# An S5 layer on one core: all 32 stacks of powers times b-bar made by GpSimd in a row, kept in DRAM and brought back

## The chip, the core and the metric

The kernel runs on one core of a Trainium2 chip. Its engines are TensorE (PE in the rows), VectorE (DVE), ScalarE (ACT), GpSimd (POOL) and SyncE (SP), which here only issues transfers. Each engine runs its own list of instructions in order and meets the others through semaphores. The metric is the device time of one execution in microseconds.

## What is computed

The reference is a two-block network on 256 latent and 256 context tokens of width 1024. The first block has an attention layer and then an S5 layer (a diagonal complex state space model, run in both directions), the second has two hybrid layers. The change touches the S5 layer alone:

```
# first_block, layer 1 (kind 1)
h = x * (1 + scale) + shift
pz = h @ s5_w_in[0];  p, z = split(pz)
y, yc = s5_mixer(p, pc, lam_re, lam_im, log_step, b_re, b_im, c_re, c_im, d, glu_w, glu_b)
x = layer_norm(alpha * x + gate * ((y * silu(z)) @ w_out[1]))
```

The mixer has 128 groups of 16 channels and 64 complex states in each direction. It discretises the diagonal matrix (a-bar) and the input matrix (b-bar). The kernel takes eight time steps at once: what eight inputs add to the state is a matrix whose blocks are the powers 7, 6, ... 0 of a-bar times b-bar. One such matrix for four groups, real and imaginary part, is called a stack here: 128 partitions x 1024 numbers, 512 KB. There are 32 stacks.

## The kernel before, in words

The program is written as stages with a method for each engine. `flow` calls the stages in one order for all engines, so the order of calls is each engine's own order. `e.mark(name)` notes, for the engine whose list is being written, the last operation that it has done so far (`self.own`). `wait_mark(name)` waits for the noted operation of all four of PE, ACT, DVE and POOL:

```
def wait_mark(self, name):
    if self.e is not None:
        for other in ("pe", "act", "dve", "pool"):
            if self.marks["plan"][name, other] is not None:
                self._ge(*self.marks["plan"][name, other])
```

The part that matters runs so. Attention ends at the mark `at1`. Then comes the output projection `OUT1` (16 x 8 tiles of weights, split into a high and a low part: ACT makes the high part, DVE the low part, PE multiplies three times), the layer norm `LN1`, and four pieces of unrelated weight work from `backlog` in each of its two gaps. Then the mark `ln1`, `Mod2` (the layer's input H), and the S5 flow, `S5.flow`.

In `S5.flow` ACT and DVE begin with `wait_mark("ln1")`. Eight projections `p0` to `p7` (two tiles of 8 + 8 matmuls 128x512 each) and sixteen tiles of `z` follow. After the first two projections the stacks are woven in two by two, in `halves(u)`: PE turns (transposes) stacks u and u + 1, does one tile of a projection (or of z, for u from 24), and then multiplies both turned stacks with the inputs (`enter`, 32 matmuls 128x64). ACT copies the turned stacks out of PSUM. For u below 16 DVE copies the product into the state buffer S, above that ACT does. SP ships each projection through DRAM into the layout that `enter` wants (`ship_sp`).

A stack takes six TENSOR_TENSOR instructions 128x512 (`stack`, line 88 for the instruction itself). GpSimd makes it, except that DVE makes the odd ones below 16 (`owner`). It lies in one of three buffers BS until PE has turned it. GpSimd loads the b-bar of each stack, 64 KB, from DRAM (`load_bb`), two buffers BB. The powers P and the factors SA are loaded once, after the mark `at1`.

When stacks 0 to 15 have entered, DVE runs the recurrence of the first half of the groups (`recur_dve`, 248 TENSOR_TENSOR 128x128 in a dependent row), and after stack 31 that of the second. After the last z tile the outputs leave, in four parts q (`leave`), with panels of tables from DRAM (`panels_sp`), and the gated linear unit follows.

Of the kernel before, what the change touches and what calls it, by code (L numbers as in the profile page):

```python
# [11 lines left out]
MUL, ADD, SUB, MAX, MIN = ALU.mult, ALU.add, ALU.subtract, ALU.max, ALU.min  # L12
# [152 lines left out]
def step(gen, n=1):  # L165
    for _ in range(n):
        next(gen, None)
# [12 lines left out]
def build(nc, I, out):  # L180
    ctx = ExitStack()
    with ctx:
# [50 lines left out]
        A = sb("A", AN)  # L233
# [350 lines left out]
        class Ada:  # L584
# [52 lines left out]
            dve = pool = none  # L637
# [85 lines left out]
        class Attention:  # L723
# [105 lines left out]
            pool = sp = none  # L829
# [211 lines left out]
        SS = S5(nc, I, dict(locals()))  # L1041
# [106 lines left out]
        def flow(e, on):  # L1148

            on(Load())  # L1150
            on(TurnIn())
            ada0, setup = on(ADA[0]), on(SS.setup)
            step(setup)
            step(ada0, 3)
            step(setup)
            step(ada0, 2)
            step(setup)
            step(ada0, 3)
            e.mark("mod1")
            on(Mod1())  # L1160
            for v in VTM:
                on(v)
            proj, backlog, tables = on(PROJ1), chain(ada0, *[on(a) for a in ADA[1:]]), on(SS.tables)
            setup = on(SS.setup2)
            for i in range(24):
                step(proj)
                step(setup)
                if i in (14, 19, 21, 23):
                    step(tables)
            on(PowersStored())  # L1170
            at = 0
            for g in range(4):
                for i, _ in enumerate(on(AT1[g])):
                    if i < 16 and g < 3:
                        step(proj)
                    else:
                        step(backlog)
                    if at % 7 in (0, 2, 4, 5):
                        step(tables)
                    elif at % 8 == 3:  # L1180
                        step(backlog)
                    at += 1
                if g == 2:
                    rest(tables)
                    on(TablesDone(SS))
            e.mark("at1")
            outp = on(OUT1)
            on(HalvesOO())
            rest(outp)
            ln = on(LN1)  # L1190
            step(ln)
            step(backlog, 4)
            step(ln)
            step(backlog, 4)
            e.mark("ln1")
            on(Mod2())
            SS.flow(e, on, backlog)
            e.mark("s5")
            on(HalvesG())
            rest(on(GLU))  # L1200
            rest(on(OUT2))
            rest(on(LN2))
            e.mark("ctx2")
            on(Ctx2())
            for L in LAYERS:
                L.flow(e, on, backlog)
            e.mark("end")
            on(FIN)
            e.mark("last")
# [48 lines left out]
class S5:  # L1258
# [5 lines left out]
    def __init__(self, nc, I, L):  # L1264
# [8 lines left out]
        def dram(name, *shape):  # L1273
            return nc.dram_tensor(name, shape, F32, kind="Internal").ap()

        self.scr = [dram(f"scr{i}", 131072) for i in range(2)]
        self.ptab, self.ctab = dram("ptab", 128, 3072), dram("ctab", 128, 128, 256)
        self.btab = dram("btab", 128, 128, 32).rearrange("g p f -> p g f")
        self.kf, self.xs = dram("kf", 128, 16, 240), dram("xs", 128, 4096)


# [18 lines left out]
        self.TM = A[:, 2560:2816].rearrange("p (x r g) -> p x r g", x=2, r=2)  # L1300
        self.P = A[:, 2816:5120]
        self.BB = [A[:, 5120 + 128 * i:5248 + 128 * i].rearrange("p (g r n) -> p g r n", g=4, r=2) for i in range(2)]
        self.BS = [[A[:, 5376 + 1024 * i + 512 * r:5888 + 1024 * i + 512 * r].rearrange("p (g j n) -> p g j n", g=4, j=8)
                    for r in range(2)] for i in range(3)]
        self.U1 = A[:, 8448:8960].rearrange("p (g j n) -> p g j n", g=4, j=8)
        self.U1D = A[:, 26368:26880].rearrange("p (g j n) -> p g j n", g=4, j=8)
        self.BM = [A[:, 8960 + 1024 * i:9984 + 1024 * i].rearrange("p (r g q) -> p r g q", r=2, g=4) for i in range(3)]
        self.US = [A[:, a:a + 2048].rearrange("p (g c) -> p g c", g=32) for a in (0, 12032, 14080, 16128)]
        self.S = [A[:, a:a + 8192].rearrange("p (s r g) -> p s r g", s=64, r=2) for a in (18176, 26368)]
# [5 lines left out]
        self.ZS = [X[:, m, 0:256] if m < 8 else A[:, 2816 + 256 * (m - 8):3072 + 256 * (m - 8)] for m in range(16)]  # L1315
        self.l_pp, self.l_bb = sig("landed_powers"), [sig(f"landed_bbar{i}") for i in range(2)]
        self.l_p, self.l_u = [[sig(f"landed_s5_{x}{i}") for i in range(n)] for x, n in (("p", 2), ("u", 4))]
        W = I["s5_w_in"][0]
        self.proj = [Lin(f"p{b}", W, 8, 256 * b, 256, lambda k: self.H[:, k, :], 512,
                         lambda k: [(self.dve_step, ("h2", k))], self.act_evac, act=self.project_act(b)) for b in range(8)]  # L1320
# [39 lines left out]
            sp.dma(self.US[q][s * 16:s * 16 + 16, 16 * i:16 * i + 16, :], src[s]).then_inc(self.l_u[q], b)  # L1360


    def owner(self, u):
        return "dve" if u < 16 and u % 2 == 1 else "pool"

    def stacked(self, u):
        return (self.dve_step if self.owner(u) == "dve" else self.pool_step), ("st", u)

    def load_bb(self, pool, u):

        if u == 0:
            pool.wait_mark("at1")
            pool.wait_ge(self.l_pt, "p")
            pool.wait_ge(self.l_bt, 1)
            pool.dma(self.P, self.ptab[:, 0:2304]).then_inc(self.l_pp, "p")
            pool.dma(self.SA, self.ptab[:, 2560:3072].rearrange("p (x r g) -> p x r g", x=2, r=2)).then_inc(self.l_pp, "p")
        elif u > 1:
            pool.wait_ge(*self.stacked(u - 2))
        pool.dma(self.BB[u % 2].rearrange("p g r n -> p g (r n)"), self.btab[:, 4 * u:4 * u + 4, :]).then_inc(self.l_bb[u % 2], u)

    def stack(self, v, u):

        if v.name == "pool":
            if u == 0:
                self.load_bb(v, 0)
            if u < 31:
                self.load_bb(v, u + 1)
        if self.owner(u) != v.name:
            return
        BR, BI = self.BS[u % 3]  # L1390
        U1 = self.U1 if v.name == "pool" else self.U1D
        s = self.pool_step if v.name == "pool" else self.dve_step

        def pw(r):
            a = self.P[:, 1152 * r:1152 * r + 1152].rearrange("p (k g) -> p g k", k=9)[:, 4 * u:4 * u + 4, 7::-1]
            return a.unsqueeze(3).to_broadcast([128, 4, 8, 16])

        def bv(r):
            return self.BB[u % 2][:, :, r, :].unsqueeze(2).to_broadcast([128, 4, 8, 16])

        v.wait_ge(self.l_pp, "p")
        v.wait_ge(self.l_bb[u % 2], u)
        if u > 2:
            v.wait_ge(self.tr_done, ("bt", u - 3))
        v.wait_own()
        v.tt(BR, pw(0), bv(0), MUL).then_inc(s)
        v.tt(U1, pw(1), bv(1), MUL).then_inc(s)
        v.wait_own()
        v.tt(BR, BR, U1, SUB).then_inc(s)
        t = v.own  # L1410
        v.tt(BI, pw(0), bv(1), MUL).then_inc(s)
        v.wait_for(t)
        v.tt(U1, pw(1), bv(0), MUL).then_inc(s)
        v.wait_own()
        v.tt(BI, BI, U1, ADD).then_inc(s, ("st", u))

    def turn_pe(self, pe, u):
        pe.wait_ge(*self.stacked(u))
        for r in range(2):
            p = self.PS.take(pe, ("bt", u, r), (self.act_evac, ("bm", u, r)))  # L1420
            for g in range(4):
                x = pe.tr(p[:, g * 128:g * 128 + 128], flat(self.BS[u % 3][r][:, g]), self.ident)
        x.then_inc(self.tr_done, ("bt", u))

    def turn_act(self, act, u):
# [175 lines left out]
                    ACT.Gelu_apprx_tanh).then_inc(self.act_step, ("gelu", q, t4))  # L1601

    def flow(self, e, on, backlog):
        own = {("ship", "sp"): self.ship_sp, ("stack", "pool"): self.stack, ("stack", "dve"): self.stack,
               ("turn", "pe"): self.turn_pe, ("turn", "act"): self.turn_act, ("enter", "pe"): self.enter_pe,
               ("enter", "act"): self.enter_act, ("enter", "dve"): self.enter_dve, ("recur", "dve"): self.recur_dve,
               ("before", "act"): self.before_act, ("before", "dve"): self.before_dve, ("panels", "sp"): self.panels_sp,
# [2 lines left out]
        def part(name, *a):  # L1610
            if (name, e.name) in own:
                own[name, e.name](e, *a)

        def halves(u, between):

            part("turn", u)
            part("turn", u + 1)
            between()
            for i in (u, u + 1):
                if i + 3 < 32:  # L1620
                    part("stack", i + 3)
                part("enter", i)

        if e.name in ("act", "dve"):
            e.wait_mark("ln1")
        for u in range(3):
            part("stack", u)
        projs, z = [on(p) for p in self.proj], on(self.z)

        def ahead(b):  # L1630

            if e.name == "sp":
                if b < 8:
                    rest(projs[b])
                else:
                    step(z, 2)

        ahead(0)
        ahead(1)
        u = 0  # L1640
        for b in range(8):
            ahead(b + 2)
# [23 lines left out]
        part("before", 1)  # L1666
        part("leave", 2)
        part("leave", 3)


def flat(a):
    return a.rearrange("p j n -> p (j n)")


class Setup:
# [387 lines left out]
class Layer:  # L2063


    def __init__(self, nc, I, L, l):
# [11 lines left out]
        nc0 = 512 - c0  # L2078
        W = I["w_in_2"][l]
        o = [0]  # L2080
# [853 lines left out]
```

## Time and profile before

| | us |
|---|---|
| median of 3 runs | 2636.81 (2636.36 to 2639.2) |
| the profiled execution | 2635.93 |
| its span in the trace | 2634.1 |
| PE busy in the span | 2220.4 (84%) |
| DVE, ACT, POOL busy | 1362.2, 906.9, 501.3 |

The span is what the trace shows from first to last instruction. The profiled execution is 1.8 us longer than it, and lies 0.9 us under the median of the runs. Times below are from the start of the span. The output projection begins at 588, the S5 flow at about 722, its last z tile ends at 1010, and its outputs have left at about 1122.

### The profile page before, as it was taken

The page shows a single profiled execution, that of the slowest core. Times are in us where ns is not written, and L with a number is a line of the kernel's source. Part 1 is how long each engine was busy: PE and PEld are TensorE (multiplying, and loading weights), DVE is VectorE, ACT ScalarE, POOL GpSimd, SP SyncE. Part 2 cuts the span into 40 slices and gives each one's busy share as a digit, 9 for nine tenths or more (in the row PEclk, how much of TensorE's full clock was granted, in tenths as well). Part 3 has the DMA queues.
Part 4 walks back from the last instruction along what each step waited for, and adds up shares of the span by engine and source line. Part 5 has one row for each costly group of instructions (what it writes and reads, how often), then busy time and mean ns, then how long its engine had stood idle before and what let it go on. Part 6 is the DMA issues. An engine that isn't in the chain of part 4 may idle for free.

```text
span 2634.1 us, 33814 instructions
## 1 busy us (share of the span) xinstructions
PE 2220.4 (84%) x13593; PEld 1674.5 (64%) x13593; DVE 1362.2 (52%) x2527; ACT 906.9 (34%) x1779; POOL 501.3 (19%) x457
## 2 busy tenths in 40 slices
PE   6878888779899775489788987879999977976998
PEld 5756666558556575389553443668888745545998
DVE  4648677553446999165334355453333223455554
ACT  3335454551212432154212344232222222344443
POOL 0047787311058950000000010000000000000000
PEclk8989999999899987699889987989999978887999
DMA  8254454793344329975322211223323442102553
GB/s 277 92 166 134 133 168 132 231 294 111 128 108 107 84 67 192 235 197 165 110 78 64 80 65 49 64 64 96 96 84 91 146 142 64 65 1 86 178 176 106
DMA packets 423666, 324.38 MB, mean 123 GB/s; under 512 B 65086, under 2 KB 411470, under 8 KB 422358
## 3 DMA queue, kind: packets, MB, share of 16 engines
q1 hardware_dynamic: 386452, 295.70, 38.7%
q10 hardware_dynamic: 34242, 16.92, 2.2%
q0 software_dynamic: 2816, 9.60, 1.1%
q8 instruction: 108, 1.77, 0.3%
q14 instruction: 48, 0.39, 0.1%
HBM read 292.42 MB, written 29.75 MB: 122 GB/s over the span
## 4 chain that ended last, share of the span: by engine, by line
PE 60%; DVE 14%; POOL 10%; DMA 6%; ACT 5%; issue 4%; SPq 1%; ACTq 1%; DVEq 0%; POOLq 0%
PE ps L119 58%; POOL A L88 9%; DVE A L88 3%; ACT A L115 3%; DMA wbuf<-ctab 2%; DVE R L88 2%; DVE A L102 2%; PE ps L122 2%; DVE A L105 1%; DVE A L92 1%; SPq L125 1%; DVE A L93 1%; POOL A L125 1%; DVE A L96 1%; DMA wbuf<-in_ada_w 1%
## 5 line engine op out<-in xcount | busy, mean ns | idle before, releaser
L119 PE MATMUL ps<-R,R 128*128 128x256 f32 (+1 forms) x3968 | 843.8, 335 | 42.6 <-ACT R L115 32.5
L119 PEld LDWEIGHTS ps<-R,R 128*128 128x128 f32 x3968 | 631.9, 194 | 125.5 <-ACT R L115 26.5
L119 PE MATMUL ps<-HR,R 128*128 128x512 f32 (+1 forms) x1984 | 562.4, 368 | 44.4 <-DVE R L88 33.2
L88 DVE TENSOR_TENSOR R<-wbuf,R 128x1024 fp32r<-128x1024 f32 (+2 forms) x304 | 333.0, 1104 | 367.6 <-ACT R L115 367.5
L119 PEld LDWEIGHTS ps<-HR,R 128*128 128x128 f32 x1984 | 354.0, 191 | 110.6 <-issue 43.9
L115 ACT ACTIVATE A<-ps 128x512 f32<-128x512 f32 (+4 forms) x400 | 210.2, 555 | 598.2 <-PE ps L119 422.1
L88 POOL TENSOR_TENSOR A<-A 128x512 f32<-128x512 f32 (+3 forms) x258 | 293.5, 1152 | 568.2 <-DVE A L96 304.3
L88 DVE TENSOR_TENSOR A<-A 128x128 f32<-128x128 f32 (+4 forms) x796 | 361.9, 485 | 63.3 <-ACT A L115 26.7
L115 ACT ACTIVATE R<-wbuf 128x1024 fp32r<-128x1024 f32 (+2 forms) x304 | 270.1, 894 | 293.8 <-PE ps L119 265.7
L119 PE MATMUL ps<-H,wbuf 128*128 128x512 f32 (+2 forms) x928 | 344.1, 530 | 22.1 <-DVE H L93 22.1
L119 PE MATMUL ps<-A 128*128 128x64 f32 (+10 forms) x1736 | 295.7, 371 | 31.1 <-DMA wbuf<-ctab 10.6
L119 PEld LDWEIGHTS ps<-H,wbuf 128*128 128x128 f32 (+1 forms) x928 | 182.1, 199 | 170.0 <-issue 146.1
L119 PEld LDWEIGHTS ps<-A 128*128 128x128 f32 (+3 forms) x1736 | 187.3, 189 | 97.1 <-issue 67.5
L122 PE MATMUL ps<-C,A 128*128 128x128 f32 (+1 forms) x663 | 107.2, 303 | 108.9 <-DVE A L92 35.1
L88 POOL TENSOR_TENSOR A<-X 128x576 f32<-128x576 f32 x128 | 165.5, 1313 | 105.1 <-ACT X L115 83.9
L122 PEld LDWEIGHTS ps<-C,A 128*128 128x128 f32 (+1 forms) x663 | 83.0, 157 | 126.1 <-issue 52.3
L125 POOL DMA_DIRECT2D A<-in_rope x3 | 1.8, 609 | 819.0 <-PE ps L119 471.0
L119 PE MATMUL ps<-A,C 128*128 128x256 f32 (+5 forms) x296 | 106.4, 510 | 51.6 <-ACT A L115 50.6
L88 DVE TENSOR_TENSOR A<-ps,A 128x256 f32<-128x256 f32 (+1 forms) x100 | 53.6, 536 | 134.1 <-PE ps L119 132.1
L115 ACT ACTIVATE R<-A 128x256 fp32r<-128x256 f32 (+1 forms) x108 | 50.1, 502 | 177.0 <-DVE A L88 176.9
L102 DVE RECIPROCAL A<-A 128x1 f32<-128x1 f32 (+4 forms) x120 | 98.4, 820 | 20.8 <-ACT A L115 18.3
L119 PEld LDWEIGHTS ps<-A,C 128*128 128x128 f32 (+2 forms) x296 | 44.6, 187 | 100.9 <-ACT A L115 60.4
(102 smaller groups left out, 1628.2 us busy)
## 6 DMA issues: line engine op xcount, KB each, us to landing
wbuf<-in_w_ada SPq DMA_DIRECT2D x48, 1024.0 KB, 6.8
wbuf<-in_ada_w SPq DMA_DIRECT2D x24, 1024.0 KB, 8.9
wbuf<-in_w_out SPq DMA_DIRECT2D x24, 1024.0 KB, 5.6
wbuf<-in_w_ffn_gate SPq DMA_DIRECT2D x22, 1024.0 KB, 5.4
wbuf<-in_w_ffn_up SPq DMA_DIRECT2D x22, 1024.0 KB, 5.4
wbuf<-in_w_ffn_down SPq DMA_DIRECT2D x32, 704.0 KB, 4.6
wbuf<-in_attn_w_in SPq DMA_DIRECT2D x20, 1024.0 KB, 7.0
ctab<-A ACTq DMA_DIRECT2D x64, 256.0 KB, 3.0
```

What stands on the lines that cost most here:

```text
L88: return self.op(lambda e: e.tensor_tensor(out, a, b, op))
L92: return self.op(lambda e: e.tensor_scalar(out, a, s1, None, op0))
L93: return self.op(lambda e: e.tensor_scalar(out, a, s1, s2, op0, op1))
L96: return self.op(lambda e: e.scalar_tensor_tensor(out=out, in0=a, scalar=s, in1=b, op0=op0, op1=op1))
L102: return self.op(lambda e: e.reciprocal(out, a))
L105: return self.op(lambda e: e.reduce_max(out, a, AX_X))
L115: return self.op(lambda e: e.activation(out, a, func, bias=bias, scale=scale))
L119: return self.op(lambda e: e.matmul(out, lhsT, rhs, start=start, stop=stop, skip_group_check=True))
L122: return self.op(lambda e: e.transpose(out, a, ident))
L125: return self.op(lambda e: e.dma_start(dst, src, allow_slow_non_contiguous=slow), 16)
```

## The change

GpSimd makes all 32 stacks in one row, `stacks(e)`, called straight after the mark `at1`, that is ahead of `OUT1` and of the mark `ln1` in its list. DVE makes none. Each finished stack is written to a DRAM tensor `bstab` by GpSimd's own queue (`spill_stack`, 512 KB); three buffers BS take turns, and a buffer is used again when its write has landed. SP brings the stacks back (`back_sp`, 512 KB each) into 13 places BL: eight in a part of A that is free then, and from stack 16 on five that lie over BS and P. `back_sp(0)` waits for the mark `ln1`; `back_sp(16)` waits for the writes of stacks 29, 30 and 31. Four stacks are asked for ahead. PE turns a stack when it is back. The rest of the flow is as it was.

```diff
             e.mark("at1")
+            if e.name == "pool":
+                SS.stacks(e)
             outp = on(OUT1)
...
+    def spill_stack(self, pool, u):
+        pool.wait_ge(self.pool_step, ("st", u))
+        pool.dma(self.bstab[u], self.BS[u % 3]).then_inc(self.l_bs[u % 3], u)
+
+    def stacks(self, pool):
+
+        pool.wait_mark("at1")
...
+        for u in range(32):
...
+            if u < 31:
+                self.load_bb(pool, u + 1)
+            pool.wait_ge(self.l_pp, "p")
+            pool.wait_ge(self.l_bb[u % 2], u)
+            if u > 2:
+                pool.wait_ge(self.l_bs[u % 3], u - 3)
+            if u:
+                pool.wait_own()
+            pool.tt(BR, pw(0), bv(0), MUL).then_inc(s)
+            pool.tt(U1, pw(1), bv(1), MUL).then_inc(s)
+            t = pool.own
+            if u:
+                self.spill_stack(pool, u - 1)
+            pool.wait_for(t)
+            pool.tt(BR, BR, U1, SUB).then_inc(s)
...
+            pool.tt(BI, BI, U1, ADD).then_inc(s, ("st", u))
+        self.spill_stack(pool, 31)
+
+    def slot(self, u):
+        return u % 8 if u < 16 else 8 + (u - 16) % 5
+
+    def back_sp(self, sp, u):
+
         if u == 0:
...
+            sp.wait_mark("ln1")
+        if u == 16:
+            for v in (29, 30, 31):
+                sp.wait_ge(self.l_bs[v % 3], v)
+        elif u >= 8 and u < 16:
+            sp.wait_ge(self.tr_done, ("bt", u - 8))
+        elif u > 20:
+            sp.wait_ge(self.tr_done, ("bt", u - 5))
+        sp.wait_ge(self.l_bs[u % 3], u)
+        sp.dma(self.BL[self.slot(u)], self.bstab[u]).then_inc(self.l_bl[self.slot(u)], u)
 
     def turn_pe(self, pe, u):
-        pe.wait_ge(*self.stacked(u))
+        pe.wait_ge(self.l_bl[self.slot(u)], u)
...
-                if i + 3 < 32:
-                    part("stack", i + 3)
+                if i + 4 < 32:
+                    part("back", i + 4)
...
-        for u in range(3):
-            part("stack", u)
...
         ahead(0)
         ahead(1)
+        for u in range(4):
+            part("back", u)
```

Where this moves instructions, the order of the built programs shows it. Lines with - are of before, with + of after. In brackets are the semaphores that an instruction waits for: `pool_step` counts GpSimd's operations, `landed_stack0` to `2` the writes of the stacks.

On ScalarE, at the start of the S5 flow: the row ahead is `Mod2`, the changed row is the first copy of projection `p0` out of PSUM.

```order
 L115 ACTIVATE X<-X 128x256 [waits dve_step] x16
-L115 ACTIVATE X<-ps 128x2x256 [waits act_step,mm_done,act_evac]
+L115 ACTIVATE X<-ps 128x2x256 [waits mm_done,act_step,pool_step,act_evac]
 L115 ACTIVATE X<-ps 128x2x256 [waits mm_done] x3
 L115 ACTIVATE A<-ps 128x512 [waits tr_done]
```

The instructions are the same; this one now waits for `pool_step` too.

On SyncE, at the same place: `wbuf<-in_s_w_in` are weights of the projections, `scr` is the DRAM tensor through which they are shipped.

```order
-L125 DMA wbuf<-in_s_w_in 128x8x256 [waits mm_done] x3
-L125 DMA scr<-X 256x1x256 [waits act_evac] x2
-L125 DMA A<-scr 16x16x64 [waits dve_step,pool_step,mm_done,landed_s5_p0]
-L125 DMA A<-scr 16x16x64 x7
+L125 DMA wbuf<-in_s_w_in 128x8x256 [waits mm_done] x2
+L125 DMA A<-bstab 128x1024 [waits pool_step,dve_step,landed_stack0,act_evac,mm_done]
+L125 DMA A<-bstab 128x1024 [waits landed_stack1]
+L125 DMA A<-bstab 128x1024 [waits landed_stack2]
+L125 DMA A<-bstab 128x1024 [waits landed_stack0]
```

Four stacks are fetched between the second and the third panel of weights, and the first of these fetches has the wait for the mark, which the first shipped load had.

On GpSimd, inside the row of stacks: stack 1 and the start of stack 2.

```order
 L125 DMA A<-btab 128x4x32 [waits pool_step]
-L125 DMA A<-btab 128x4x32 [waits dve_step]
+L88 TENSOR_TENSOR A<-A 128x512 [waits landed_bbar1]
+L88 TENSOR_TENSOR A<-A 128x512
+L125 DMA bstab<-A 128x1024
+L88 TENSOR_TENSOR A<-A 128x512 [waits pool_step]
+L88 TENSOR_TENSOR A<-A 128x512
+L88 TENSOR_TENSOR A<-A 128x512 [waits pool_step] x2
+L125 DMA A<-btab 128x4x32 [waits pool_step]
```

The wait for DVE's stack is gone, and a 512 KB write stands between the second and the third operation of each stack.

## Rows read from the trace of the kernel before

**Rows 1.** The page: the span, and the chain that ended last, by engine.

```profile
span 2634.1 us, 33814 instructions
...
PE 60%; DVE 14%; POOL 10%; DMA 6%; ACT 5%; issue 4%; SPq 1%; ACTq 1%; DVEq 0%; POOLq 0%
```

**Rows 2.** Stretches: engine busy us and counts, granted TensorE clock, DMA share.

```profile
core 0: us, PE busy (x) PEld busy (x) DVE busy (x) ACT busy (x) POOL busy (x), PEclk, DMA share, GB/s
588.40:722.00 133.60, 123.21 (x588) 89.47 (x588) 51.22 (x77) 33.28 (x66) 10.95 (x7) 0.93 0.38 119
...
746.00:843.00 97.00, 97.00 (x514) 66.39 (x513) 58.43 (x87) 21.86 (x41) 66.34 (x63) 1.00 0.40 100
843.00:958.70 115.70, 85.88 (x457) 64.56 (x455) 113.71 (x116) 50.43 (x80) 108.08 (x96) 0.88 0.29 76
1010.00:1060.00 50.00, 22.75 (x412) 18.83 (x416) 46.73 (x191) 14.65 (x15) 0.00 (x0) 0.66 0.99 216
```

**Rows 3.** Timeline of PE: start us, us, instruction, count, idle before and releaser.

```profile
716.82 29.11 PE L119 MATMUL ps<-H,wbuf 128*128 128x512 f32 x64 [8.44 <-DVE H L93]
745.76 1.91 PE L122 MATMUL ps<-C,A 128*128 128x128 f32 x16
747.51 7.03 PE L119 MATMUL ps<-H,wbuf 128*128 128x512 f32 x16
...
842.87 1.92 PE L122 MATMUL ps<-C,A 128*128 128x128 f32 x16
...
859.44 8.73 PE L119 MATMUL ps<-H,wbuf 128*128 128x512 f32 x16
...
909.31 3.62 PE L119 MATMUL ps<-H,wbuf 128*128 128x256 f32 x16
...
968.21 41.66 PE L119 MATMUL ps<-H,wbuf 128*128 128x256 f32 x192
...
1074.42 2.79 PE L119 MATMUL ps<-A 128*32 128x128 f32 x48 [7.47 <-DMA A<-ctab]
```

**Rows 4.** Waits of PE from 720 to 970: total us, times, longest.

```profile
PE ps L122 <- POOL A L88: 29.9, 8, 7.3
```

**Rows 5.** Timeline of GpSimd: stack 0, a b-bar load, stacks 17 and 18.

```profile
588.39 10.32 POOL L88 TENSOR_TENSOR A<-A 128x512 f32<-128x512 f32 x6 [7.22 <-DMA A<-btab]
599.01 0.79 POOL L125 DMA_DIRECT2D A<-btab  x1 [0.29 <-POOL A L88]
...
834.93 6.99 POOL L88 TENSOR_TENSOR A<-A 128x512 f32<-128x512 f32 x6
...
843.01 7.10 POOL L88 TENSOR_TENSOR A<-A 128x512 f32<-128x512 f32 x6
```

**Rows 6.** VectorE beside stack 0 (timeline), and its low parts from 600 to 700 (group).

```profile
588.32 3.50 DVE L88 TENSOR_TENSOR R<-wbuf,R 128x1024 fp32r<-128x1024 f32 x3
597.74 2.05 DVE L88 TENSOR_TENSOR R<-wbuf,R 128x1024 fp32r<-128x1024 f32 x1 [5.93 <-ACT R L115]
...
L88 DVE TENSOR_TENSOR R<-wbuf,R 128x1024 fp32r<-128x1024 f32 x12 | 14.7, 1226 | 26.6 <-ACT R L115 26.6
```

**Rows 7.** VectorE in two stretches of the recurrences: us, busy us, count.

```profile
846.00:958.00 112.00, 110.10 (x112) 0.88 0.28 75
995.00:1060.00 65.00, 60.77 (x248) 0.74 0.93 205
```

**Rows 8.** GpSimd's loads of powers, 560 to 960: count, busy us, mean ns.

```profile
L125 POOL DMA_DIRECT2D A<-ptab x2 | 1.1, 572 | 88.6 <-DVE A L88 88.6
```

**Rows 9.** DMA issues, 578 to 700, then 720 to 960: KB each, us to landing.

```profile
A<-btab POOLq DMA_DIRECT2D x3, 64.0 KB, 8.0
...
wbuf<-in_s_w_in SPq DMA_DIRECT2D x10, 1024.0 KB, 6.2
scr<-X SPq DMA_DIRECT2D x16, 256.0 KB, 2.5
A<-scr SPq DMA_DIRECT2D x64, 64.0 KB, 3.0
```

More of the change, by code:

```diff
@@ L1278, in __init__ @@
         self.btab = dram("btab", 128, 128, 32).rearrange("g p f -> p g f")
+        self.bstab = dram("bstab", 32, 128, 1024)
         self.kf, self.xs = dram("kf", 128, 16, 240), dram("xs", 128, 4096)
@@ L1302, in __init__ @@
         self.BB = [A[:, 5120 + 128 * i:5248 + 128 * i].rearrange("p (g r n) -> p g r n", g=4, r=2) for i in range(2)]
-        self.BS = [[A[:, 5376 + 1024 * i + 512 * r:5888 + 1024 * i + 512 * r].rearrange("p (g j n) -> p g j n", g=4, j=8)
-                    for r in range(2)] for i in range(3)]
+        self.BS = [A[:, 5376 + 1024 * i:6400 + 1024 * i] for i in range(3)]
+        self.BL = [A[:, a:a + 1024] for a in [26368 + 1024 * i for i in range(8)] + [5376, 6400, 7424, 2816, 3840]]
         self.U1 = A[:, 8448:8960].rearrange("p (g j n) -> p g j n", g=4, j=8)
-        self.U1D = A[:, 26368:26880].rearrange("p (g j n) -> p g j n", g=4, j=8)
         self.BM = [A[:, 8960 + 1024 * i:9984 + 1024 * i].rearrange("p (r g q) -> p r g q", r=2, g=4) for i in range(3)]
@@ L1317, in __init__ @@
         self.l_p, self.l_u = [[sig(f"landed_s5_{x}{i}") for i in range(n)] for x, n in (("p", 2), ("u", 4))]
+        self.l_bs = [sig(f"landed_stack{i}") for i in range(3)]
+        self.l_bl = [sig(f"landed_stack_back{i}") for i in range(13)]
         W = I["s5_w_in"][0]
@@ L1360, in ship_sp @@
             sp.dma(self.US[q][s * 16:s * 16 + 16, 16 * i:16 * i + 16, :], src[s]).then_inc(self.l_u[q], b)
[L1363 to L1367, printed above, removed]
     def load_bb(self, pool, u):
-        if u == 0:
[L1372 to L1415, printed above, removed]
@@ new lines, in load_bb, with pw, bv @@
+        if u > 1:
+            pool.wait_ge(self.pool_step, ("st", u - 2))
+        pool.dma(self.BB[u % 2].rearrange("p g r n -> p g (r n)"), self.btab[:, 4 * u:4 * u + 4, :]).then_inc(self.l_bb[u % 2], u)
+    def spill_stack(self, pool, u):
[3 more added lines that the diff above has]
+        pool.wait_mark("at1")
+        pool.wait_ge(self.l_pt, "p")
+        pool.wait_ge(self.l_bt, 1)
+        pool.dma(self.P, self.ptab[:, 0:2304]).then_inc(self.l_pp, "p")
+        pool.dma(self.SA, self.ptab[:, 2560:3072].rearrange("p (x r g) -> p x r g", x=2, r=2)).then_inc(self.l_pp, "p")
+        self.load_bb(pool, 0)
+        for u in range(32):
+            BR, BI = [self.BS[u % 3][:, 512 * r:512 * r + 512].rearrange("p (g j n) -> p g j n", g=4, j=8) for r in range(2)]
+            U1, s = self.U1, self.pool_step
+            def pw(r):
+                a = self.P[:, 1152 * r:1152 * r + 1152].rearrange("p (k g) -> p g k", k=9)[:, 4 * u:4 * u + 4, 7::-1]
+                return a.unsqueeze(3).to_broadcast([128, 4, 8, 16])
+            def bv(r):
+                return self.BB[u % 2][:, :, r, :].unsqueeze(2).to_broadcast([128, 4, 8, 16])
+            if u < 31:
[13 more added lines that the diff above has]
+            pool.tt(BR, BR, U1, SUB).then_inc(s)
+            t = pool.own
+            pool.tt(BI, pw(0), bv(1), MUL).then_inc(s)
+            pool.wait_for(t)
+            pool.tt(U1, pw(1), bv(0), MUL).then_inc(s)
+            pool.wait_own()
+            pool.tt(BI, BI, U1, ADD).then_inc(s, ("st", u))
+        self.spill_stack(pool, 31)
@@ L1421, in turn_pe @@
             for g in range(4):
-                x = pe.tr(p[:, g * 128:g * 128 + 128], flat(self.BS[u % 3][r][:, g]), self.ident)
+                a = 512 * r + 128 * g
+                x = pe.tr(p[:, g * 128:g * 128 + 128], self.BL[self.slot(u)][:, a:a + 128], self.ident)
         x.then_inc(self.tr_done, ("bt", u))
@@ L1603, in flow @@
     def flow(self, e, on, backlog):
-        own = {("ship", "sp"): self.ship_sp, ("stack", "pool"): self.stack, ("stack", "dve"): self.stack,
+        own = {("ship", "sp"): self.ship_sp, ("back", "sp"): self.back_sp,
                ("turn", "pe"): self.turn_pe, ("turn", "act"): self.turn_act, ("enter", "pe"): self.enter_pe,
@@ L1668, in flow @@
         part("leave", 3)
-def flat(a):
-    return a.rearrange("p j n -> p (j n)")
 class Setup:
```

## The prediction

> **What bounds the kernel now.** I read the page first: PE is on the chain that ended last for 60% of the span and GpSimd for 10% [rows 1]. 10% is some 260 us, as long as the S5 flow, so the flow was to be read by stretches and then engine by engine.
>
> The reader should see two regimes. From 746 to 843 PE is busy for all of 97.0 us [rows 2]: although the chain names GpSimd, PE has no idle time there. Turns of stacks 0 and 1 begin at 745.76 and those of 16 and 17 at 842.87 [rows 3], eight pairs in 97.1 us, 12.14 us a pair. Stacks made faster give nothing there. From 843 to 958.7 PE is busy for only 85.9 of 115.7 us [rows 2], and its waits for GpSimd sum to 29.9 us in 8 waits [rows 4]; the rest of what is lost is a lower clock after such waits (granted 0.88; a projection tile of 8.73 us where it takes 7.03) [rows 2, 3]. After that the last twelve z tiles end at 968.21 + 41.66 = 1009.9 [rows 3].
>
> The undisturbed length of the flow, from the first turn to the last z tile, is then 12 pairs with a projection tile at 12.14 (145.7), 4 pairs with a z tile at 12.14 - 7.03 + 3.62 = 8.73 (34.9) and 41.7 for the rest [rows 3]: 222.3 us. Before it took 1009.9 - 745.8 = 264.1. So **41.8 us** is all that stacks on time can give, if everything else stays. What follows (the outputs, paced by DMA: DMA share 0.99 from 1010 to 1060 [rows 2]) is chained behind the last z tile and moves with it.
>
> **What the change does to the order: the term that decides.** GpSimd's row of stacks stands in its list before the mark `ln1`. The mark notes each engine's last operation so far. Before, GpSimd's was the last operation of the tables: 2 memsets and 32 x 6 operations, count 194. Now it is the last operation of stack 31, count 194 + 192 = 386. Everyone who waits for `ln1` now waits for **all 32 stacks**: ACT ahead of its first copy out of PSUM in the flow, DVE ahead of its first copy, SP ahead of the first stack brought back, as the changed rows of ACT and SP in the section on the change show. Behind ACT's wait are queued all copies of projections and turned stacks; behind SP's the third panel and all shipping; PE waits for stack 0 to be back. PE can do the first four projection tiles (29.1 us from 716.8 [rows 3]) and then stands. Let G be the time when stack 31 is finished. Nothing in the flow goes on before G.
>
> **G, step by step.** Stack 0 starts at 588.39 as before and takes 10.32 us; the next b-bar load is issued from 599.01 for 0.79 us [rows 5], so stack 1 starts at 599.8. In an unbroken row the start-to-start time is 843.01 - 834.93 = 8.08 us (six operations 6.99, the rest one b-bar load with its gap) [rows 5]. Each further stack also issues a write. A load of 9 KB a partition took 0.57 us of GpSimd's issue [rows 8], a b-bar load with many small pieces 0.79 with 0.29 of gap [rows 5]. The write has one piece a partition, so I take 0.57 and a gap of 0.2: 0.78. Its lower end is 0 (hidden in the wait between operations 2 and 3), its upper 1.08. A stack is then 8.86 us (8.08 to 9.16). Stack 31 starts 30 x 8.86 = 265.8 later, at 865.6, and ends 6.99 + 0.78 later: 873.4 (849 to 883).
>
> To this comes VectorE's share of the memory. Stack 0 took 10.32 where another takes 6.99: 3.3 us more, beside 3.50 us of VectorE's low parts; at 597.74 it is VectorE that takes 2.05 for 1.23 [rows 5, 6]. So one waits for the other. Twelve more low parts of 1.23 us, 14.7 together [rows 6], now meet GpSimd, and in LN1 some dozens of short operations, which I put at the same again (an estimate: DVE's 51.2 busy us of 588 to 722 [rows 2] less the low parts and what reads PSUM). In the other direction stands 846 to 958, where VectorE did 112 operations in 112 us and GpSimd's stacks took 7.10, hardly more than 6.99 [rows 5, 7]: there VectorE paid. I take 14 us, half of the 29, with the ends 0 and 29. **G = 887** (849 to 912).
>
> The Trainium skill, page "SBUF — State Buffer", section "SBUF: two separate sides", says that VectorE operations with two SBUF inputs and GpSimd operations share one port pair, and that whichever starts first gets it for the whole instruction while the other fully blocks. This speaks against moving the stacks beside the low parts. By it GpSimd could lose the full 29 us and the time would be some 15 us above my forecast; the trace agrees in kind at stack 0 (3.3 us lost beside 3.50) but not in amount at the recurrences.
>
> **From G to the end.** The first stack comes back 512 KB later: 256 KB land in 2.5 us and 1 MB in 6.2 [rows 9], so about 3.7, after an issue of about half a us: turn 0 at G + 4. The first `enter` also needs the projections shipped, which used to run under the other projections: ACT's two copies and four issues of stacks ahead (G + 2), two writes that land behind 2 MB of stacks (to about G + 9), eight loads issued over 3.8 us and landed 3.0 later [rows 9]: G + 15.8, where PE would be ready at 4 + 1.9 + 7.0 = 13 (15 on the low clock). Call it 8 us from G to the point that answers to 745.8, with ends 4 and 14. Then 222.3 us: the last z tile ends at G + 230.3 = **1117**, against 1009.9: **+107.4 us**.
>
> What hides the rest. LN1's operations on VectorE get slower beside GpSimd by up to some 15 us, and PE's four projection tiles start so much later: covered, since PE has 887 - 746 = 141 us to spare. The low parts in `OUT1` are made while PE still multiplies earlier groups (three buffers); a wait for GpSimd of some 0.8 us each (2.05 for 1.23 [rows 6]) should be hidden, and if it were not, 12 x 0.8 = 10 us still lie within the 141. The recurrences: with GpSimd quiet, 248 operations take 65 us, where beside GpSimd 112 took 112 us [rows 7]. The first starts at G + 8 + 100 and ends at G + 173, the second starts after stack 31 has entered (about G + 190) and ends at G + 255; the outputs that need it start 64.5 us after the last z tile before (1074.42 - 1009.9 [rows 3]), here at G + 295. So it has 40 us of slack and gives nothing. DVE's eight stacks left out lie beside PE-bound work: nothing. The added transfers: 16 MB of writes at 0.5 MB in 8.9 us, and 16 MB back at 1 MB per pair of 12.1 us, some 85 GB/s on top of 100, below the 216 GB/s that were reached [rows 2]: nothing. `back_sp(16)`, which waits for stacks 29 to 31, finds them done.
>
> Sum: 2635.9 (the profiled execution) + 107.4 = **2743 us**, 4% above the median of 2636.8, which lies 0.9 us above that execution.
>
> **Rivals.**
> 1. The hold at `ln1` does not bite and the flow starts at 746 as before. For it speaks only that the text of the flow itself is unchanged; against it that the first rows of ACT, DVE and SP now wait for `pool_step`. Then `back_sp(16)` is the gate: stack 16 is back at G + 5 = 892 instead of turned at 843, then 222.3 - 97.1 = 125.2 us remain: 1017, +7 us, **2643**. With the lowest G of 849 it is 979, -31 us, 2605: this is the way to **faster**, and it gives faster if G is below about 875. The same holds if G itself were below 780 (then G + 230 < 1010), but that wants 5.8 us a stack, under the 6.99 of its operations alone.
> 2. GpSimd is throttled by its transfers. b-bar loads landed in 8.0 us while the large weight loads ran [rows 9]; a stack gives them 8.9. If the writes on the same queue push them to 11, some 12 to 14 stacks take 3 us more: +40, **2783**. A write itself has two stacks' time, 15 us.
> 3. GpSimd's writes cost nothing and VectorE always gives way: G = 849, **2706**.
>
> **How the numbers follow.** Forecast 2743: chance 0.80 with its own spread. Rival 1: 0.04, split between no change, faster and slower. Rival 2: 0.09. Rival 3, exactly at its end: 0.07. The ends are -24 to +9 for the writes (31 x the ends of 8.08 and 9.16 against 8.86), -14 to +15 for the port, -4 to +6 for the restart; taken together without adding all of one sign: 2715 to 2775. A difference of 0.2% (5 us) is about what a measurement of this kernel can tell from no change. Faster by more than that 0.02, within it 0.01, slower 0.97.
>
> **What would show it.** Right: GpSimd works without a gap from 588 to about 887; ACT has one idle time of over 140 us ended by GpSimd, PE one of about 130 ended by the stack brought back; after it the flow takes about 225 us with PE hardly waiting, pairs 12.1 us apart; the recurrences take 65 us each. Wrong: if ACT copies the first projection tile at 725 as before, the reading of the mark is wrong. If stacks are 8.1 or 9.5 us apart instead of 8.9, the size is off by 31 times the difference. If PE waits inside the flow for stacks brought back, the restart or the transfers were underrated.

## The result and the profile after

The changed kernel takes 2732.79 us (median of 4 runs, 2730.11 to 2736.5) against 2636.59 before: ratio 1.0367, 95% interval 1.0347 to 1.0388. It is 96 us slower. 2743 was forecast, with 2715 to 2775 as the range. The profiled execution took 2730.11, its span is 2728.3, 94.2 us longer than that of before [rows 1].

The page, the span and the chain that ended last by engine and by line:

```profile
span 2728.3 us, 33885 instructions
...
PE 61%; DVE 13%; POOL 12%; DMA 6%; ACT 4%; issue 2%; SPq 1%; ACTq 0%; DVEq 0%; POOLq 0%
```

ScalarE around the mark `ln1` (timeline: start, us, instruction, count, idle before and its releaser):

```profile
775.56 0.42 ACT L115 ACTIVATE X<-X 128x256 f32<-128x256 f32 x1 [2.56 <-DVE H L93]
874.52 2.06 ACT L115 ACTIVATE X<-ps 128x512 f32<-128x512 f32 x4 [98.55 <-POOL A L88]
```

This is the hold. The last scaling of `Mod2` ends at 776; then ScalarE is idle for 98.55 us, released by GpSimd, and copies four projection tiles in a row that have long waited in PSUM. The forecast said over 140 us for this idle time and about 130 for PE's; they are 98.6 and 79.2, because LN1 and H took 54 us longer than before and G came 13 us earlier. SyncE shows the same from its side, its queue's issues:

```profile
702.90 1.91 SPq L125 DMA_DIRECT2D wbuf<-in_s_w_in  x2
874.60 2.07 SPq L125 DMA_DIRECT2D A<-bstab  x4
876.71 0.77 SPq L125 DMA_DIRECT2D wbuf<-in_s_w_in  x1
877.53 3.77 SPq L125 DMA_DIRECT2D scr<-X  x2
888.17 3.76 SPq L125 DMA_DIRECT2D A<-scr  x8
```

GpSimd's row, stack 1, the end of the last b-bar load, and stack 31:

```profile
600.90 2.20 POOL L88 TENSOR_TENSOR A<-A 128x512 f32<-128x512 f32 x2
603.03 0.60 POOL L125 DMA_DIRECT2D bstab<-A  x1
603.64 5.68 POOL L88 TENSOR_TENSOR A<-A 128x512 f32<-128x512 f32 x4
...
841.41 0.80 POOL L125 DMA_DIRECT2D A<-btab  x1 [0.29 <-POOL A L88]
...
849.98 0.80 POOL L125 DMA_DIRECT2D A<-btab  x1 [0.29 <-POOL A L88]
...
866.97 2.16 POOL L88 TENSOR_TENSOR A<-A 128x512 f32<-128x512 f32 x2 [0.17 <-POOL A L88]
869.08 0.61 POOL L125 DMA_DIRECT2D bstab<-A  x1
869.71 4.73 POOL L88 TENSOR_TENSOR A<-A 128x512 f32<-128x512 f32 x4
```

It never waits for a transfer or for another engine; its only gaps are short ones behind its own operations, mostly of 0.3 us and at most 0.6. Stack 31 ends at 874.4, and ScalarE and SyncE start 0.1 and 0.2 us later. TensorE after that (timeline), where [rows 3] is the same of before:

```profile
775.58 24.08 PE L119 MATMUL ps<-H,wbuf 128*128 128x512 f32 x50 [1.23 <-DVE H L93]
878.81 1.97 PE L122 MATMUL ps<-C,A 128*128 128x128 f32 x8 [79.16 <-DMA A<-bstab]
881.57 1.97 PE L122 MATMUL ps<-C,A 128*128 128x128 f32 x8 [0.80 <-DMA A<-bstab]
886.97 10.09 PE L119 MATMUL ps<-H,wbuf 128*128 128x512 f32 x16 [3.43 <-DMA wbuf<-in_s_w_in]
896.90 3.68 PE L119 MATMUL ps<-A 128*128 128x64 f32 x32
900.42 1.92 PE L122 MATMUL ps<-C,A 128*128 128x128 f32 x16
...
1033.95 1.92 PE L122 MATMUL ps<-C,A 128*128 128x128 f32 x16
...
1068.86 41.66 PE L119 MATMUL ps<-H,wbuf 128*128 128x256 f32 x192
```

PE stands for 79 us. From 900.42 to 1033.95 eleven pairs pass in 133.5 us, 12.14 a pair, without a wait. The last z tile ends at 1068.86 + 41.66 = 1110.5, against 1009.9.

What the forecast had far too small is beside the path here, but it decides some of the experiments. VectorE's groups of the second half of LN1 and of H, by form: first before (706 to 722), then after (706 to 776); count, busy us, mean ns:

```profile
L88 DVE TENSOR_TENSOR X<-X,A 128x512 f32<-128x512 f32 x8 | 5.5, 686 | 0.0
L93 DVE TENSOR_SCALAR H<-X,MOD 128x256 f32<-128x256 f32 x16 | 5.3, 414 | 0.0
L93 DVE TENSOR_SCALAR X<-X,VT 128x512 f32<-128x512 f32 x8 | 4.4, 546 | 0.3
```

```profile
L93 DVE TENSOR_SCALAR H<-X,MOD 128x256 f32<-128x256 f32 x16 | 34.2, 2213 | 0.0
L88 DVE TENSOR_TENSOR X<-X,A 128x512 f32<-128x512 f32 x8 | 18.9, 2357 | 0.0
L93 DVE TENSOR_SCALAR X<-X,VT 128x512 f32<-128x512 f32 x8 | 16.1, 2014 | 0.3
```

15.2 us became 69.2. GpSimd stood still there before, and its row runs through all of it after.

### The profile page after: what moved, and what is told of

Its sections match the earlier page's. It is cut to its first block, busy times and chain, and to the rows that moved or that the text cites. A ratio compares the mean times of both kernels' runs of the same rounds, so it can differ in the third digit from the quotient of the medians.

```text
span 2728.3 us, 33885 instructions
## 1 busy us (share of the span) xinstructions
PE 2219.6 (81%) x13593; PEld 1667.9 (61%) x13593; DVE 1313.9 (48%) x2479; ACT 907.8 (33%) x1779; POOL 580.4 (21%) x537
## 4 chain that ended last, share of the span: by engine, by line
PE 61%; DVE 13%; POOL 12%; DMA 6%; ACT 4%; issue 2%; SPq 1%; ACTq 0%; DVEq 0%; POOLq 0%
PE ps L119 58%; POOL A L88 11%; PE ps L122 3%; DVE A L88 2%; ACT A L115 2%; DMA wbuf<-ctab 2%; DVE A L102 2%; DVE R L88 2%; DVE A L92 2%; DVE A L105 1%; DVE A L93 1%; SPq L125 1%; POOL A L125 1%; DMA wbuf<-in_w_ada 1%; DMA wbuf<-in_ada_w 1%
## 5 line engine op out<-in xcount | busy, mean ns | idle before, releaser
L88 DVE TENSOR_TENSOR R<-wbuf,R 128x1024 fp32r<-128x1024 f32 (+2 forms) x304 | 344.4, 1141 | 361.7 <-ACT R L115 361.7
L88 POOL TENSOR_TENSOR A<-A 128x512 f32<-128x512 f32 (+3 forms) x306 | 353.0, 1169 | 560.9 <-DVE A L96 304.5
L119 PE MATMUL ps<-H,wbuf 128*128 128x512 f32 (+2 forms) x928 | 350.9, 536 | 68.7 <-DVE H L93 65.3
L88 DVE TENSOR_TENSOR A<-A 128x128 f32<-128x128 f32 (+4 forms) x748 | 244.5, 356 | 57.2 <-ACT A L115 44.1
L119 PEld LDWEIGHTS ps<-A 128*128 128x128 f32 (+3 forms) x1736 | 183.8, 185 | 92.5 <-issue 59.5
L99 DVE COPY A<-ps 128x128 f32<-128x128 f32 (+4 forms) x95 | 49.4, 547 | 272.7 <-PE ps L119 258.4
```

The lines of the kernel that those rows point to most:

```text
L88: return self.op(lambda e: e.tensor_tensor(out, a, b, op))
L99: return self.op(lambda e: e.tensor_copy(out, a))
L119: return self.op(lambda e: e.matmul(out, lhsT, rhs, start=start, stop=stop, skip_group_check=True))
```

## The experiments

The theory to test: the time of GpSimd's row sets the result through the hold at `ln1`. The rivals: the trip through DRAM and SyncE's longer queue, or VectorE disturbed by GpSimd. The kernel before was run beside each batch on the same chip (2635.96 us for e1, e4, e5 and e6, and 2634.74 for the others).

| run | median us | ratio to before, 95% | last z tile ends |
|---|---|---|---|
| e2_short_stacks | 2607.82 | 0.9900 (0.9875 to 0.9925) | 979.5 |
| e1_mark_free | 2647.29 | 1.0050 (1.0032 to 1.0068) | 1024.4 |
| e4_mark_free_pause | 2651.84 | 1.0074 (1.0049 to 1.0100) | 1026.9 |
| e6_places_no_pause | 2635.87 | 1.0014 (0.9989 to 1.0040) | 1022.5 |
| e5_places_pause | 2607.96 | 0.9905 (0.9876 to 0.9935) | 985.1 |
| e7_places_pause2 | 2597.01 | 0.9863 (0.9838 to 0.9888) | 979.3 |
| e8_h_by_act | 2618.74 | 0.9939 (0.9918 to 0.9959) | 993.0 |
| e3_no_dve_alone | 2658.61 | 1.0087 (1.0061 to 1.0113) | not used |

The last column is from the profiled execution, which is not always near the median: it took 2652.5 us for e1, 2648.8 for e4, 2614.9 for e5 and 2647.1 for e6.

**e2: only GpSimd's time.** Hold, DRAM, queue and order stay; four of a stack's six operations go.

```diff
             pool.tt(BR, pw(0), bv(0), MUL).then_inc(s)
-            pool.tt(U1, pw(1), bv(1), MUL).then_inc(s)
-            t = pool.own
             if u:
                 self.spill_stack(pool, u - 1)
...
-            pool.tt(BR, BR, U1, SUB).then_inc(s)
...
-            pool.tt(BI, pw(0), bv(1), MUL).then_inc(s)
...
-            pool.tt(BI, BI, U1, ADD).then_inc(s, ("st", u))
+            pool.tt(BI, pw(0), bv(1), MUL).then_inc(s, ("st", u))
```

> The changed kernel as it is, hold at ln1 and trip through DRAM included, but each stack is made of two of its six operations (the products with the imaginary parts are left out, so the output is not the reference's). Theory (the time that GpSimd's row takes is the cost, nothing else): a stack takes about 4 us, the row ends at about 720, LN1 is stretched only until then, the first turn comes at 750 to 762 and the last z tile at 972 to 985: 2600 to 2612 us, under the kernel before. Rival (trip through DRAM, SyncE's queue with 32 more fetches, or the order of waits): well above 2636, toward 2733.

Measured 2607.8. The row ends at 727.6, PE has no wait for a stack at all, and the time is 125 us under that of the changed kernel, more than the 96 us that the change costs, with nothing changed but the row's length. So the trip through DRAM, 32 more fetches on SyncE and the order of waits cost nothing that shows. What is left beside the row, LN1 stretched until 727.6, shows: PE's four projection tiles start at 728.2, not at 716.8.

**e1: only the hold.**

```diff
+                held = e.own
                 SS.stacks(e)
...
             e.mark("ln1")
+            if e.name == "pool":
+                e.marks["ln1", "pool"] = held
```

> The changed kernel, but the mark ln1 notes GpSimd's last operation ahead of its row of stacks, so nobody waits for the whole row there. Theory (the hold at ln1 is the cost, GpSimd's pace behind it): ACT, DVE and SP go on when LN1 is done. LN1 and the writing of H are still stretched beside GpSimd as in the changed kernel (H finished at 775.5, first four projection tiles at 799.7), so the first turn is at about 800, and 222.3 us later the last z tile at 1022, against 1009.9 before and 1110.5 with the change: about 2648 us. The fetch of stack 16, which waits for the whole row (875 us), is then no gate (turn 16 at 897). Rival (the port shared by GpSimd and VectorE, or the trip through DRAM and SyncE's longer queue, is the cost): the time stays near 2733.

Measured 2647.3 against 2648 expected. TensorE of e1 (timeline), then its waits from 690 to 1030 (total us, times, longest):

```profile
749.27 2.05 PE L119 MATMUL ps<-H,wbuf 128*128 128x512 f32 x2 [37.64 <-DVE H L93]
...
778.22 24.10 PE L119 MATMUL ps<-H,wbuf 128*128 128x512 f32 x50 [1.23 <-DVE H L93]
802.16 1.91 PE L122 MATMUL ps<-C,A 128*128 128x128 f32 x16
...
982.74 41.66 PE L119 MATMUL ps<-H,wbuf 128*128 128x256 f32 x192
```

```profile
PE ps L119 <- DVE H L93: 52.1, 8, 37.6
```

From the first turn at 802.2 to 1024.4 are 222.2 us: the flow is bound by PE throughout, its gain of 42 us is there. It is more than eaten by the later start (802.2 against 745.8), nearly all of it the 54 us of LN1 and H ahead of it. The hold alone was worth 2732.8 - 2647.3 = 85 us.

**e4: the hold, and LN1 undisturbed.**

```diff
+            if u == 12:
+                pool.wait_ge(self.dve_step, ("h2", 7))
```

> As e1, and GpSimd stops after 12 stacks (about 702 us) until VectorE has written H, so LN1 is not disturbed. Theory: the first turn is back at 746, but the row ends 15 to 20 us later, at about 893, and the fetch of stack 16 waits for it: turn 16 at 897 instead of 843, last z tile at 897 + 125 = 1022, about 2649 us, the same as e1 by another wait. Rival (disturbing LN1 is what e1 still loses): 12 us less than e1, about 2636 or below.

Measured 2651.8, no better than e1. TensorE of e4 (timeline):

```profile
716.54 29.16 PE L119 MATMUL ps<-H,wbuf 128*128 128x512 f32 x64 [8.43 <-DVE H L93]
...
899.77 3.67 PE L122 MATMUL ps<-C,A 128*128 128x128 f32 x16 [56.95 <-DMA A<-bstab]
```

The flow starts on time, and then waits 57 us for stack 16, since `back_sp(16)` waits for the whole row (893). One wait has taken the place of another of the same size. This is the gate of the first rival of the forecast, seen alone.

**e6 and e5: places that don't lie over GpSimd's buffers.** Stacks 16 to 27 come back into one former buffer BS, one former BM and two halves of a US block that is filled later; only 28 to 31 wait for the row. GpSimd and ACT have two buffers BS and BM left instead of three, and the fetches of stacks 22 to 27 are asked for two ahead. e5 has the pause of e4 as well, e6 has not.

```diff
-        self.BL = [A[:, a:a + 1024] for a in [26368 + 1024 * i for i in range(8)] + [5376, 6400, 7424, 2816, 3840]]
+        self.BL = [A[:, a:a + 1024] for a in [26368 + 1024 * i for i in range(8)]
+                   + [11008, 7424, 16128, 17152, 5376, 6400, 2816, 3840]]
...
-        return u % 8 if u < 16 else 8 + (u - 16) % 5
+        return u % 8 if u < 16 else u - 8 if u < 20 else 8 + u % 2 if u < 28 else u - 16
...
-        if u == 16:
-            for v in (29, 30, 31):
+        if u == 28:
+            for v in (30, 31):
```

> As e5 without the pause: GpSimd's row runs through LN1. Theory: LN1 and H stretched as in the changed kernel, first turn at 800, last z tile at 1022: about 2648 us, so the places alone give nothing and pause and places only pay together. Rival (GpSimd beside LN1 costs nothing on the path): as e5.

> As e4, and the stacks from 16 on come back into places that don't lie over GpSimd's buffers and powers (one buffer BS, one buffer BM and a part of US given up for them), so the fetch of stack 16 no longer waits for the whole row; only stacks 28 to 31 do. Theory: neither wait is left and PE bounds the whole flow: 222.3 us from 746, last z tile at 968, 41 us less than before: 2595 to 2602 us, faster than both kernels. Rival (DMA or ScalarE or the recurrences beside GpSimd take over): PE waits for stacks brought back or for copies, 2615 or more.

e6 came out at 2635.9: no difference from before, 12 us under the expectation of 2648, and 11 under e1. The expectation was off by more than the noise. It took e6's row for that of the changed kernel, and it is not: with two buffers BS GpSimd waits for its own writes, which it never did with three. GpSimd's waits of e6 from 588 to 910:

```profile
POOL A L88 <- DMA bstab<-A: 12.3, 7, 3.0
```

In that profiled execution the three groups of LN1 and H took 62.6 us, against 69.3 in e1 and 15.2 before, and PE waited 3.5 us for stacks 28 and 29. Whether such pauses account for all of the 12 us is not shown. Nor is what spreads e6's ten runs, from 2628 to 2656, more than those of before; the profiled one, with 2647.1, is among the slow three. What e6 does show is that the places without the pause give nothing against the kernel before.

e5 measured 2608.0, 28 us less than before but 6 above its expectation. TensorE of e5:

```profile
908.62 1.97 PE L122 MATMUL ps<-C,A 128*128 128x128 f32 x8 [4.61 <-DMA A<-bstab]
915.22 1.97 PE L122 MATMUL ps<-C,A 128*128 128x128 f32 x8 [4.63 <-DMA A<-bstab]
```

The row ends only at 904.2, 7.7 us of it in waits for its own writes, and stacks 28 and 29 waited for it.

**e7: as e5, with stacks 28 and 29 in the two free places too.**

```diff
-        return u % 8 if u < 16 else u - 8 if u < 20 else 8 + u % 2 if u < 28 else u - 16
+        return u % 8 if u < 16 else u - 8 if u < 20 else 8 + u % 2 if u < 30 else u - 18
...
-        if u == 28:
+        if u == 30:
...
```

The cut above is against e5. Stacks 28 and 29 are also asked for two ahead, and 30 and 31 together.

> The fifth kernel waited 4.6 us each for stacks 28 and 29, which came back only when GpSimd's whole row was done (904). Here 28 and 29 use the two free places too, and only 30 and 31 wait for the row. Theory: PE bounds all of the flow, the 13 us that the fifth kernel still lost go down to a few, last z tile 972 to 975 where the row of weights starts 3.4 us late as there, 2595 to 2600 us. Rival (two places are too few at 8.7 us a pair): PE waits for 26 to 29 instead, no gain over the fifth, 2608.

Measured **2597.0**, ratio 0.9863 (0.9838 to 0.9888): faster than both kernels. PE, and VectorE's two recurrences:

```profile
720.55 29.10 PE L119 MATMUL ps<-H,wbuf 128*128 128x512 f32 x64 [8.43 <-DVE H L93]
...
908.52 3.68 PE L122 MATMUL ps<-C,A 128*128 128x128 f32 x16 [3.97 <-DMA A<-bstab]
...
937.66 41.66 PE L119 MATMUL ps<-H,wbuf 128*128 128x256 f32 x192
```

```profile
849.46 173.74 DVE L88 TENSOR_TENSOR A<-A 128x128 f32<-128x128 f32 x496
```

From the first turn at 749.5 to 979.3 are 229.8 us, 7.5 above the undisturbed 222.3. Of the 41.8 us that the forecast found in the flow 34.3 are had. It starts 3.7 us later than before, a lateness that was there before LN1, so the last z tile is 30.6 us earlier. The span is 38.9 us shorter and the medians differ by 37.7, so some 8 us came behind the flow. The recurrences end at 1023.2, and the outputs that need them start at 1043.1, behind a wait for a table, so they hold nothing up.

**e8: who is held up in LN1.** e6 with H written by ScalarE.

```diff
-                        dve.ts(H[:, k, sl], X[:, k, sl], M[:, 8 + k, s:s + 1], M[:, k, s:s + 1], MUL, ADD
-                               ).then_inc(dve_step, ("h2", k, s), ("h2", k))
+                        act.act(H[:, k, sl], X[:, k, sl], ACT.Identity, bias=M[:, k, s:s + 1], scale=M[:, 8 + k, s:s + 1]
+                                ).then_inc(act_step, ("h2", k, s), ("h2", k))
```

> The sixth kernel (row of stacks through LN1, no waits for the row up to stack 28) with H written by ScalarE instead of VectorE. Theory (what stretches LN1 and H by 54 us is that VectorE's operations on the memory are held up by GpSimd's): ScalarE's 16 operations take their usual 0.33 us and follow LN1's pairs of 8.9 us; H is complete at about 742 instead of 768 to 775, PE ends its first four tiles at about 750 to 755, last z tile about 975: 2600 to 2606 us. Rival (the memory as a whole, or the clock, is slow beside GpSimd): ScalarE's operations are stretched as well, 2635 or more.

Measured 2618.7: under e6 (ratios 0.9939 and 1.0014), but 13 above the upper end expected. ScalarE of e8, while GpSimd's row runs on (with two buffers, so with seven waits for its writes, 11.3 us in all):

```profile
733.37 1.09 ACT L115 ACTIVATE H<-X,MOD 128x256 f32<-128x256 f32 x2 [2.21 <-DVE X L93]
738.97 1.09 ACT L115 ACTIVATE H<-X,MOD 128x256 f32<-128x256 f32 x2 [4.51 <-DVE X L93]
```

Two operations take 1.09 us and wait only for VectorE; VectorE took 2.2 us for one. ScalarE's sixteen scalings of X behind them took 4.99 us in a row beside GpSimd, and 5.26 before. So it is VectorE's operations that are held, not every reader of the memory. The 1.09 for two is more than the 0.33 for one that I had expected, which was the time of a scaling; no run has this form with GpSimd quiet. The price was off because I let PE finish its four tiles soon after H: H was complete at 740, but 50 of the 64 matmuls were still to do (to 763.8), as each tile needs all of H. From there to 993.0 are 229.2 us, 7 more than undisturbed, with 4.5 us of waits for stacks 28 and 29 among them.

**e3: VectorE's share alone.** In the kernel before, `owner` gives all stacks to GpSimd.

```diff
-        return "dve" if u < 16 and u % 2 == 1 else "pool"
+        return "pool"
```

> The kernel before with one part of the change alone: VectorE makes no stack, GpSimd makes all 32 in the flow, no DRAM, no new order. Theory: GpSimd bounds the flow from 726 on at 8.1 to 8.3 us a stack: stack 31 done at 726 + 31 x 8.2 = 980 instead of 958.7, about 2654 to 2660 us; so the eight stacks that the change takes from VectorE are worth about 20 us when they are not made early. Rival (VectorE's stacks were hidden, so they cost nothing elsewhere): 2637.

Measured 2658.6, 24 us more, as expected. PE's waits for GpSimd from 690 to 1000 are now 45.6 us in 13 waits [29.9 in 8, rows 4]:

```profile
PE ps L122 <- POOL A L88: 45.6, 13, 6.5
```

## Why the forecast was right, point by point

**The hold: right.** GpSimd's last operation ahead of the mark became that of stack 31. ScalarE's idle time ended by GpSimd, SyncE's first fetch 0.2 us after the row and e1, which takes away this wait alone and 85 us with it, show it. e2 shows that nothing else of what the change adds costs anything once the row is short.

**G: 874.4, forecast 887 (849 to 912).** Two terms of the sum were sized too large. The write was put at 0.78 us; it costs 0.60 of issue and no gap, and the rest of a stack takes 0.1 us less than in [rows 5]: undisturbed stacks follow at 849.98 - 841.41 = 8.57 us, not 8.86, which is 9 us over 31 stacks. The port was put at 14 us; the row lost 9.9. Stack 31 starts at 866.97, 266.1 us after 600.90; undisturbed this would be 29 x 8.57 and 7.61 for stack 30, after which no b-bar load comes, 256.1. Some 8 of the 9.9 us were lost beside the weights' low parts, 1.4 in LN1. The Trainium skill's rule (page "SBUF — State Buffer", section "SBUF: two separate sides"), that whoever starts first blocks the other for a whole instruction, held in kind: VectorE's low parts took up to 3.58 us where 1.23 is usual [rows 6]. The 2.35 us more are longer than one GpSimd operation of 1.1 us, so VectorE did not always get through behind the first. Who loses more in the long run was not equal: GpSimd, with a stream of dependent operations of 1.1 us, lost 9.9 us, and VectorE 54 us in LN1 and H alone, and 12 in the low parts (32.6 us for 20.3, from 588 to 706).

**Restart: 14 us, forecast 8 (4 to 14), the upper end.** Stack 0 was back at G + 4.4 as said. The step that was priced too low is the queue behind SyncE's hold, in two ways. The one that ended last: the third weight panel, named in the forecast as queued there but given no price, was issued only behind four stacks, PE waited 3.4 us more for it, and did the tile on a lower clock (granted 0.70 from 887 to 897; 10.09 us for 7.03). Close behind it came the shipping: its loads were issued from 888.2, which is G + 13.8 where G + 9 was said, the last of them from 891.5, and they land some 3 us after their issue, so `enter` could not have begun before some 894.5 either (an estimate from these), G + 20 where G + 15.8 was said. SyncE had stood 6.9 us for the shipped tiles to be written, behind the 2 MB of stacks and the panel.

**The flow: 222.2 us, forecast 222.3** (from 888.3, which is 896.9 less the 8.6 from a first turn to its `enter` in the other pairs, to 1110.5; the time lost before 896.9 is counted in the restart). The recurrences took 65.4 us each with 17.9 us between them, with slack, as forecast.

**The sum.** Last z tile 1110.5 instead of 1117: 12.6 less for G, 6 more for the restart. From there to the end the changed kernel gained 6.4 us more (+100.6 at the last z tile, +94.2 over the span). This is not in the forecast and lies far behind the change: where the layer's outputs have left (1120.9 in the kernel before) TensorE is still 100.3 us later, at 2300 it is 97, at 2325 it is 92.5. e7, compared with the same profiled execution of before, gains the same 4.5 us between 2300 and 2325. Why was not traced. The profiled execution came out 13 us under the forecast of 2743: 7 are the two terms above, of opposite sign, and 6 no step of the forecast covers.

**What was covered, and was wrong.** The forecast let LN1 stretch by up to 15 us; it was 54. The forecast's own rows had the factor: [rows 7] has 112 operations of the recurrences in 112 us beside GpSimd and 248 in 65 us without it, 3.8 times as long for each. The forecast read there that VectorE paid, and did not carry the price over to LN1. By that factor the 15.2 us would have become 58; they became 69. It cost nothing in the changed kernel, because all of it lay under the hold, but it is the whole loss of e1. The first rival had this wrong: with the hold gone it named the fetch of stack 16 as the gate, and in e1 that fetch is late for nobody, since LN1 has already lost as much. Only with LN1 undisturbed (e4) does the gate bite.

**The rivals.** Transfers did not throttle GpSimd: writes landed in some 3 us where two stacks' time was there, b-bar loads in some 2.4 us where [rows 9] has 8.0, and GpSimd waited for none of them in the row. This margin hangs on the three buffers: with two (e5 to e8) it waited for writes, 7.7 to 12.3 us in all. The low end (writes free, port free, G = 849) was not reached either.

## What to carry to other kernels

A wait on "all that this engine has done so far" changes its meaning when work is put ahead of it in that engine's list: before moving work past such a mark, list who waits for it and what they need from that engine (here nothing: naming the older operation gave back 85 us). Work moved to an idle engine is not free where it shares the memory with an engine on the path: the same row cost TensorE 0.8 us beside `OUT1` (382 matmuls in 89.43 us, 88.62 before), where VectorE had slack, and 54 us beside LN1. And with several waits of the same size in a row, taking away one more of them shows little (against the kernel before, e1, e4 and e6 are all between no gain and a loss of 16 us); only all three together (e7) gave 38 us, near the 42 that the profile of before had promised.

## What was not expected of the hardware

Beside a dense stream of GpSimd operations, VectorE gets through only at a few points: 16 operations of 0.41 us took 34.2 us, four in each of GpSimd's 8.57 us stacks. Operations with a single tensor in SBUF as input (the TENSOR_SCALAR of LN1 and H) were held as well as those with two; those that read one tensor from PSUM were not (the sixteen residuals of `OUT1`, with GpSimd quiet before and busy after, took 480 ns on the mean in both; the six copies of `enter` for a pair took 4.3 us with GpSimd busy before and quiet after). ScalarE's scalings were not held (e8). GpSimd's own loss in the whole row of 285 us was 3.4 us in stack 0 (10.37 for 6.99) and 9.9 after it.
